# Attention scores as one joint product and two others, sample products over all partitions, and pooling history turned once a tile

## What is computed

```python
xn = rms_norm(h, norm_g)
u, zp, q, k, v, za, ga, gb = split(xn @ w_in)                 # 1024 x 6656
ya = multiscale_pool(concat(pool_prev, u)) * silu(zp)         # windows 2, 4, 8, 16
new_pool = concat(pool_prev, u)[:, -15:]                      # the last 15 rows
q, k = rope(rms_norm(q)), rope(rms_norm(k))                   # 16 query, 4 key heads of 64
o = softmax_with_sink(q @ k.T, window of 128) @ v
m = sigmoid(ga) * (ya @ w_proj_pool) + sigmoid(gb) * ((o * silu(za)) @ w_proj_attn)
h = h + m @ w_out
h = h + sigmoid(h @ w_ple_gate) * (p @ w_ple)
```

## Time and profile before

| | |
|---|---|
| median of 3 runs | 1165.45 us |
| the profiled execution's own time | 1165.09 us |
| its span in the trace | 1163.3 us |
| granted TensorE clock, mean | 0.999 of full |
| busy: PE products | 1156.3 us (99%), 7656 products |
| busy: DVE | 563.9 us (48%) |
| busy: ACT | 395.9 us (34%) |
| busy: POOL | 407.7 us (35%) |

### The profile page before, as it was taken

One profiled execution on the slowest core, in us unless ns is written; L12 is line 12 of the kernel. 1 busy time (PEld: TensorE's weight loads), 2 busy tenths in 40 slices (PEclk: granted clock), 3 DMA queues, 4 the chain that ended last, 5 costly groups with the idle time before them and its releaser, 6 DMA issues.

```text
span 1163.3 us, 20002 instructions
## 1 busy us (share of the span) xinstructions
PE 1156.3 (99%) x7656; PEld 1143.1 (98%) x7656; DVE 563.9 (48%) x1045; ACT 395.9 (34%) x954; POOL 407.7 (35%) x191
## 2 busy tenths in 40 slices
PE   8999999999999999999999999999999999999998
PEld 8999999999999999999999999999999999999998
DVE  5566774112556566564726465832363451163322
ACT  6433334233766767666110010321321030031112
POOL 4433332333212222223333344335432532374310
PEclk9999999999999999999999999999999999999999
DMA  9425466313455555652611111072223232412211
GB/s 303 168 73 149 141 165 181 94 46 87 132 154 158 153 154 134 166 148 74 218 54 51 37 50 36 23 276 76 92 75 124 82 124 77 135 65 64 65 38 56
DMA packets 145791, 130.83 MB, mean 112 GB/s; under 512 B 49039, under 2 KB 134439, under 8 KB 145727
## 3 DMA queue, kind: packets, MB, share of 16 engines
q1 hardware_dynamic: 131063, 106.21, 30.0%
q10 hardware_dynamic: 14664, 23.74, 7.1%
HBM read 94.82 MB, written 37.12 MB: 113 GB/s over the span
## 4 chain that ended last, share of the span: by engine, by line
PE 99%; DMA 1%; SPq 0%; DVE 0%; issue 0%; DVEq 0%
PE ps L684 75%; PE ps L822 11%; PE ps L933 2%; PE ps L708 2%; PE ps L1092 1%; PE ps L964 1%; PE ps L947 1%; PE ps L784 1%; PE ps L698 1%; PE ps L968 1%; PE ps L951 1%; PE ps L1061 1%; DMA xr<-in_x_prompt 1%; PE ps L888 0%; PE ps L868 0%; PE ps L1040 0%
## 5 line engine op out<-in xcount | busy, mean ns | idle before, releaser
L684 PE MATMUL ps<-m_hi,w_hi 128*128 128x352 f32 x1704 | 556.1, 327 | 0.1
L684 PE MATMUL ps<-m_lo,w_hi 128*128 128x352 f32 x1704 | 548.1, 322 | 0.0
L684 PE MATMUL ps<-m_hi,w_lo 128*128 128x352 f32 x1704 | 369.8, 325 | 0.0
L684 PEld LDWEIGHTS ps<-m_hi,w_hi 128*128 128x128 f32 x1704 | 320.9, 188 | 1.3 <-issue 0.5
L684 PEld LDWEIGHTS ps<-m_lo,w_hi 128*128 128x128 f32 x1704 | 320.7, 188 | 0.0
L597 POOL TENSOR_TENSOR w_hi<-raw_a,w_one 128x1024 fp32r<-128x1024 f32 x41 | 78.9, 1923 | 683.4 <-PE ps L684 371.4
L684 PEld LDWEIGHTS ps<-m_hi,w_lo 128*128 128x128 f32 x1704 | 289.8, 188 | 0.0
L599 POOL TENSOR_TENSOR w_lo<-raw_b,w_hi 128x1024 fp32r<-128x1024 f32 x41 | 111.1, 2709 | 3.2
L599 POOL TENSOR_TENSOR w_lo<-raw_a,w_hi 128x1024 fp32r<-128x1024 f32 x41 | 104.1, 2539 | 3.2
L822 PE MATMUL ps<-w_lo,m_hi 128*128 128x256 f32 (+1 forms) x360 | 99.4, 282 | 0.0
L822 PE MATMUL ps<-w_hi,m_hi 128*128 128x256 f32 x320 | 92.3, 288 | 0.0
(11 more groups left out here) (248 smaller groups left out, 1429.9 us busy)
## 6 DMA issues: line engine op xcount, KB each, us to landing
raw_a<-in_w_in SPq DMA_DIRECT2D x25, 512.0 KB, 3.7
raw_b<-in_w_in SPq DMA_DIRECT2D x25, 512.0 KB, 4.6
qk_d<-qkst ACTq DMA_DIRECT2D x20, 512.0 KB, 5.6
gate_d<-gst ACTq DMA_DIRECT2D x16, 528.0 KB, 3.4
gin<-gate_d SPq DMA_DIRECT2D x16, 528.0 KB, 3.6
qt<-qk_d SPq DMA_DIRECT2D x64, 128.0 KB, 3.5
kt<-qk_d SPq DMA_DIRECT2D x96, 64.0 KB, 2.5
vt<-v_d SPq DMA_DIRECT2D x84, 64.0 KB, 2.2
```

Source lines behind the costliest of these rows:

```text
L684: last = nc.tensor.matmul(ps[:, 3 * parity + c, 0:CH], w, x[:, k, CH * c:CH * c + CH], start=(k == 0 and w is wh and x is src_hi), stop=(k ...
```

## The change

Scores: `kt` has two slots by unit parity, each with three planes of 256 tokens: plane 0 holds the high parts of the keys on both halves of the partitions, plane 1 the low parts on the lower half only, plane 2 the low parts on the upper half only; the rest is zero. A new tile `q_high` holds the high parts of q for heads b = 0 on the lower half and b = 1 on the upper half. One product of `q_high` with planes 1 and 2 (2 x 192 columns) replaces the two products with low parts; the two with plane 0 stay. DVE fills `q_high` in a new step `stack_high`, for the next unit, and PE waits for it. DVE's loop over the attention has one pass fewer, which is written out.

Samples: L870 and L885 run over all 128 partitions, with zeros where there was nothing. History: only the 4 new rows of each sample are turned, beside the 15 rows of the prompt, in one transpose; the rows are collected in `kv_flat` and stored at the end by SP; the 11 old rows go from input to output directly. The samples' rows of p are padded to 128 for their transposes.

The diff is cut; the left-out parts are the constants of waits and the matching zero fills on ACT (`v_group`, `spt`, `q_sum`).

```diff
-            kt = sb("kt", [P, NKV, 2, 3, P], F32R, scope=s3)
+            kt = sb("kt", [P, 2, 3, 2 * P], F32R, scope=s3)
+            k_gap = sb("k_gap", [P, 1024], scope=s3)
+            q_high = sb("q_high", [P, 2, 2, 2, HD], F32R, scope=s3)
...
+            sp.dma_start(pool_rows(npool_s)[:, 0:HIST - NT, :], pool_rows(state)[:, NT:HIST, :]).then_inc(out_stored, 16)
...
-                for slot in ((2, 0) if m < 4 else (1,)):
-                    for half in range(2):
-                        sp.dma_start(kt[HD * half:HD * half + HD, kv, :, slot, :].bitcast(F32),
-                                     qk_d[NH + kv, :, tok].rearrange("(s e) n -> e s n", s=2))\
-                            .then_inc(unit_loaded[kv], 16)
+                seen = slice(0, P) if first else bass.ds(t * P - P, 2 * P)
+                for half in range(2):
+                    dst = kt[HD * half:HD * half + HD, m % 2, 0:2 + half:1 + half, P if first else 0:2 * P]
+                    sp.dma_start(dst.bitcast(F32), qk_d[NH + kv, :, seen].rearrange("(s e) n -> e s n", s=2))\
+                        .then_inc(unit_loaded[kv], 16)
...
+            sp.wait_ge(zero_done, 1)
             for m in range(2):
                 load_q_k(m, 0, m)
...
+                sp.wait_ge(pool_copied, KT + 1)
+                sp.dma_start(npool_p, kv_flat[NS:NS + HIST, 0:D]).then_inc(pool_stored, 16)
+                for b in range(NB):
+                    sp.dma_start(pool_rows(npool_s)[b, HIST - NT:HIST, :], kv_flat[NT * b:NT * b + NT, 0:D])\
+                        .then_inc(pool_stored, 16)
...
+                sp.dma_start(yrow[NS:P, PBLK, :], pp[NS:P, :]).then_inc(p_loaded, 16)
...
-                nc.tensor.matmul(ps[:, 7, P:SK], q_sum[0:HD, P * v:P * v + P], k_new[0:HD, NS * v:NS * v + NS],
+                nc.tensor.matmul(ps[:, 7, P:SK], q_sum[:, P * v:P * v + P], k_new[:, NS * v:NS * v + NS],
...
-                nc.tensor.matmul(ps[:, 7, 0:P], v_group[0:NS].rearrange("p s e -> p (s e)"), spt[0:NS, 1, :],
+                nc.tensor.matmul(ps[:, 7, 0:P], v_group[:].rearrange("p s e -> p (s e)"), spt[:, 1, :],
...
+                    pe.wait_ge(q_high_put, u + 1)
                 bank = round_of("S", u, s, m, first)
+                seen = slice(HD * s, HD * s + KW)
+                nc.tensor.matmul(ps[:, bank, :].rearrange("p (b n) -> p b n", b=2)[:, :, 0:KW],
+                                 q_high[:, slot, s, :, :].rearrange("p g n -> p (g n)"), kt[:, slot, 1:3, seen],
+                                 start=True, stop=False)
                 for b in range(2):
-                    for part in range(2):
-                        keys = kt[:, kv, part, :, :].rearrange("p s n -> p (s n)")[:, k0:k0 + KW]
-                        last = nc.tensor.matmul(ps[:, bank, 256 * b:256 * b + KW],
-                                                qt[:, slot, s, 2 * b:2 * b + 2, :].rearrange("p g n -> p (g n)"), keys,
-                                                start=(part == 0), stop=(part == 1))
+                    last = nc.tensor.matmul(ps[:, bank, 256 * b:256 * b + KW],
+                                            qt[:, slot, s, 2 * b:2 * b + 2, :].rearrange("p g n -> p (g n)"),
+                                            kt[:, slot, 0, seen], start=False, stop=(b == 1))
...
-                nc.tensor.transpose(ps[0:nh, 6, 0:P], keep[:, h, :], ident)
-                nc.tensor.transpose(ps[0:HIST, 6, P:2 * P], ub[:, h, SEQ:SEQ + HIST], ident).then_inc(pool_t, 1)
+                nc.tensor.transpose(ps[0:nh, 6, 0:P], keep[:, h, :], ident).then_inc(pool_t, 1)
...
-                    last = nc.tensor.transpose(ps[:, 6 + r % 2, 0:NS], yrow[0:NS, PBLK, P * k:P * k + P],
-                                               ident[0:NS, 0:NS])
+                    last = nc.tensor.transpose(ps[:, 6 + r % 2, 0:P], yrow[:, PBLK, P * k:P * k + P], ident)
...
+            def stack_high(m, t):
+
+                dve.wait_ge(unit_loaded[m % 4], t * 64 + 64)
+                for b in range(2):
+                    last = v.tensor_copy(q_high[HD * b:HD * b + HD, m % 2, :, :, :],
+                                         qt[0:HD, m % 2, :, 2 * b:2 * b + 2, :].bitcast(F32))
+                last.then_inc(q_high_put, 1)
...
-                    v.memset(kt[:, :, :, 1, :].bitcast(F32), 0.0).then_inc(zero_done, 1)
+                    v.memset(kt[:].bitcast(F32), 0.0).then_inc(zero_done, 1)
...
                 step.did(v.memset(sst[:, 0:1], 0.0))
+                if last_group:
+                    stack_high(0, 0)
                 scale_za(kv, 1)
...
                     split_probs(u - 1, (m - 1) % 8)
+                if not (isinstance(i, int) and u == PBLK * NKV - 1):
+                    stack_high((m + 1) % 8, i * 2 + (m + 1) // 4)
                 reciprocals(u, m)
...
-                    ge(dve, pool_t, 2 * g + h - 1)
+                    ge(dve, keep_ready, 2 * g + h - 1)
...
-            dve.wait_ge(pool_stored, 16 * 2 * KT)
...
             scale_gin(0, 5)
+            dve.wait_ge(pool_stored, 16 * (NB + 1))
...
-                ge(act, pool_stored, 32 * (k))
-                a.activation(pst[0:nh, 0, :], ps[0:nh, 6, 0:P], ACT.Copy)
-                a.activation(pst[0:HIST, 1, :], ps[0:HIST, 6, P:2 * P], ACT.Copy).then_inc(pool_copied, 1)
-                act.wait_ge(pool_copied, need + 1)
-                cols = bass.ds(k * P, P)
-                act.dma_start(npool_s[:, cols], pst[0:nh, 0, :]).then_inc(pool_stored, 16)
-                act.dma_start(npool_p[:, cols], pst[0:HIST, 1, :]).then_inc(pool_stored, 16)
+                a.activation(kv_flat[0:NS + HIST, bass.ds(k * P, P)], ps[0:NS + HIST, 6, 0:P], ACT.Copy)\
+                    .then_inc(pool_copied, 1)
```

More of the change, by code:

```diff
@@ L330, in build @@
         att_done, att_read = sem("att_done"), sem("att_read")
-        low_copied, low_added = sem("low_copied"), sem("low_added")
+        low_copied, low_added, q_high_put = sem("low_copied"), sem("low_added"), sem("q_high_put")
         masks_loaded, zero_done = sem("masks_loaded"), sem("zero_done")
@@ L358, in build @@
         v_low, gtmp, sg = kv_out[0:HD, 0, :], kv_flat, rbc
-        pst = kv_out[:, 0, 0:2 * P].rearrange("p (a n) -> p a n", n=P)
         rms_rows = [rows[0:P if t < PBLK else NS, 4, P * t:P * t + P] for t in range(PBLK + 1)]
@@ L382, in _, with pool_rows @@
         def _(sp):
+            def pool_rows(ap):
+                return ap.rearrange("(b h) n -> b h n", h=HIST)
             def load_chunk(n, w, col, extra=None, extra_n=None):
@@ L462, in load_q_k @@
             def load_q_k(u, t, m):
-                tok, kv = bass.ds(t * P, P), m % 4
+                kv = m % 4
                 for a in range(2):
@@ L467, in load_q_k @@
                         .then_inc(unit_loaded[kv], 16)
-                for slot in ((2, 0) if m < 4 else (1,)):
-                    for half in range(2):
-                        sp.dma_start(kt[HD * half:HD * half + HD, kv, :, slot, :].bitcast(F32),
-                                     qk_d[NH + kv, :, tok].rearrange("(s e) n -> e s n", s=2))\
-                            .then_inc(unit_loaded[kv], 16)
+                first = isinstance(t, int) and t == 0
+                seen = slice(0, P) if first else bass.ds(t * P - P, 2 * P)
[3 more added lines that the diff above has]
+                        .then_inc(unit_loaded[kv], 16)
             v_rows = v_d.rearrange("b p v e -> (b p) v e")
@@ L581, in _ @@
             sp.dma_start(y_s[:, 7 * P:8 * P], yrow[0:NS, PBLK, P:2 * P]).then_inc(y_stored[1], 16)
-            sp.wait_ge(out_stored, 16 * (2 * NB + 2 + 2 * NB))
+            sp.wait_ge(out_stored, 16 * (2 * NB + 3 + 2 * NB))
         @block.gpsimd
@@ L919, in round_of, with scores @@
                 return 6 + (att_bank(kind, m, first) + s) % 2
-            def scores(u, m, i, s, first=False):
+            def scores(u, m, t, s, first=False):
                 slot, kv = m % 2, m % 4
@@ L975, in attention_half @@
                 after, between = {k0: [], k0 + 1: [], k0 + 2: [], k0 + 3: []}, {}
-                after[k0].append(lambda: scores(u, m, i, 0, first and m == 0))
-                after[k0 + 1].append(lambda: scores(u, m, i, 1, first and m == 0))
+                after[k0].append(lambda: scores(u, m, t, 0, first and m == 0))
+                after[k0 + 1].append(lambda: scores(u, m, t, 1, first and m == 0))
                 if not first or m >= 1:
@@ L1036, in turn_p @@
                 k, i = divmod(r, 3)
-                pe.wait_ge(p_loaded, 16 * (PBLK + 1))
+                pe.wait_ge(p_loaded, 16 * (PBLK + 2))
                 ge(pe, p_round_free, r - 1)
@@ L1323, in _ @@
             dve.wait_ge(masks_loaded, 16)
-            dve.wait_ge(out_stored, 16 * (2 * NB + 2 + 2 * NB))
+            dve.wait_ge(out_stored, 16 * (2 * NB + 3 + 2 * NB))
             def mask_scores(u, m, start, first):
@@ L1387, in _ @@
                 attention_half(0, m, first=True)
-            with dve.Fori(1, PBLK // 2) as i:
```

(17 more changed lines are left out.)

3 lines of the change are left out of this document (1 added, 2 removed).

## The result

The changed kernel takes 1182.86 us in the median of four executions (1179.02 to 1183.86), the kernel before 1165.12 beside it. The ratio is 1.0145, 95% interval 1.012 to 1.0169: slower by 1.45%, 17.7 us. The profiled execution took 1182.12 us (span 1180.3, granted clock 0.994), 17.0 more than the one of before (1165.09).

A forecast was written before the change was run, and what follows sets the result against it. TensorE, busy 99% of the span, was taken as the bound: 1165.1 - 6.6 gained + 5.0 for held copies + 3.5 for the first pair = 1167.0, plus 0.4 for the median: 1167.5 us, range 1159 to 1182.

The forecast's parts named there:

- double hold: Rival at every fourth unit: POOL wins and queues its next instruction between DVE's two copies; 18.2 us, total 1181.5; chance 0.28.
- the tie: Every fourth unit: POOL's split and DVE's first copy start nearly together, POOL 0.05 ahead; given to neither.
- single hold: Forecast case, every fourth unit: only the second copy waits for POOL; 0.8 each, 0.5 at seams, 5.0 us; 1167.5, chance 0.50.
- the release from DVE's end to PE's start: Delay from the end of DVE's copies to PE's next scores, taken as 0.48 us from L1305 and the scores.
- The first stack_high: First copy pair, after the last sample values, between L1305 and the scores: 0.7 to 4.4 us, taken as 3.5.
- behind L599: Case for the program's first copy pair: it waits for POOL's L599, costing PE 2.7 us.
- The gains: PE time saved: scores 3.1, L870 0.9, L885 1.2, transposes of p 0.5, history 0.9; 6.6 us.
- The round's 0.048: Scores: a round falls from 0.45 to 0.40 us, saving 0.048 in each of 64 rounds, 3.1 us.
- L885's 0.31: Sample product with 32 active rows: full partitions give back 0.31 us, four times, 1.2 us.
- The bare formula: Scores products at columns / 2.4 + 2.5 ns: only 2.5 ns saved each round, 0.16 us in all.
- The parts put at nothing: K loads, state rows, late SP stores, ScalarE's clears, larger kt clear, DVE's store wait: all covered, no cost.
- The signs named: Expected in the profile: 192 scores products, PE waits near 286 and every fourth unit; 3 us waits mean both copies held.

The follow-up runs named there:

- pair_split: Changed kernel, but at every fourth unit the first q_high copy goes between the two parts of the probability split, the second behind it: 1162.77 us, ratio 0.9983.
- act_copies: Changed kernel with q_high copies on ScalarE at each unit's head, first pair on DVE ahead of the last sample product's wait: 1156.58 us, ratio 0.9931.
- four_products: Changed kernel with scores by the four 192-column products of the kernel before, without q_high copies or their wait: 1160.57 us, ratio 0.9964.
- after_again: The changed kernel as it is, measured again beside the kernel before on another chip: 1181.24 us, ratio 1.0147.

## Why the prediction was wrong

It forecast 1167.5 us and a range to 1182; the time was 1182.86, within 1.4 us of the rival of the double hold (1181.5), which had 0.28. The mechanism of that rival is what happened; that its number is so near is partly luck, since it priced the holds at 22.6 us where they cost 18.25, and had no term for the clock, which cost 6.2.

- **The step that failed** is the tie: "that 0.05 ahead is enough no row shows, so I give the tie to neither", and then the chance went nearly two to one to the single hold (0.50 against 0.28), whose 5.0 us stood in the sum. POOL was 0.05 ahead at these places (457.02 against 457.07) and won six of the seven with both of its instructions; the seventh, where DVE was ahead, as the text had it ("0.05 behind once"), was the one single hold. The rows of the tie were right to 0.02 us; the order that they showed should have been followed. Copies asked for 0.03 after the split with POOL 0.02 ahead of the split's end come second, in each of the six.
- **The price of the double hold** was near: 18.2 us for the seven places, 15.95 measured there (2.4 and 2.7 for 2.7 and 3.0). The ends of the copies were right (4.43 after the split for 4.4). Too long was the release from DVE's end to PE's start, 0.48 in the text, which had said that it need not be a pure wait: it took 0.14 (461.47 to 461.61). The whole difference of 0.3 at a place is that. The mechanism, one POOL instruction for each of the two copies, was as described. The Trainium skill (SBUF — State Buffer, Who interferes with whom) has it as an exclusive lock, first come first served; the trace agrees, down to 0.05 us.
- **The price of the single hold** was too high by the same 0.3: 0.8 against 0.47 in the change (2.2 + 0.14 - 1.87), and less in pair_split. Had the tie fallen the other way, the kernel would have been, as an estimate from these sizes, at 1165.1 - 7.7 + 7 x 0.47 + 2.3 = 1163.0 and no slower.
- **The first stack_high** was sized at 3.5 between ends of 0.7 and 4.4; it cost 2.3, the case "behind L599" (2.7) with the same 0.3 off.
- **The gains** were 6.6 by the sum and 7.7 in the trace, 7.9 in act_copies. The round's 0.048 became 0.053. Two errors met there: the new round was put at 0.40 with 0.112 for each small product, where one takes 0.087, and without the 0.02 that the product behind loses as before; with both it is 0.40 again. L885's 0.31 became 0.39: of the sample records on full partitions the 32-column ones take 0.03 from start to start. The bare formula of the Trainium skill (TensorE: Matmul & The Clock Gate, Back-to-back issue gap), by which 0.16 us would have come, is off here by almost 4 us (act_copies against four_products: 4.0); its own warning holds.
- **What was missing altogether** is the clock. The text used 0.999 and never asked what a standstill does to it. It cost 6.2 us in the profiled execution, and put the time past the end of the range: the sum of the double hold with the sizes measured is 1165.1 - 7.7 + 18.25 = 1175.7, and the clock and the 0.1 behind each hold bring it to 1182.
- **The parts put at nothing** (K loads, state copy, late stores, clears) were nothing or nearly so: none has a row among PE's waits, and four_products, which has them all, is faster by 3.9 us, where the starts of its products give 4.3.
- **The signs named** came: waits of 3 us (2.5) at every fourth unit, released by the copy, 192 products on the scores lines, a first wait near 286.

## What to carry to other kernels

A short SBUF copy put on VectorE can cost the GpSimd instruction that runs at that moment, and the next copy the next one: look for the GpSimd instruction that starts within 0.1 us of the new copy's place and take the order of the records at its word. Here both engines hang on PE, and they met in the recorded order at all seven places, with margins of 0.05 and 0.03 us. Before a wait is blamed, see what else stands behind the held instruction on its engine; here most of the loss came back a round later when the wait was gone. Put such a copy on an engine that isn't held (ScalarE, 0.42 us each instead of 2.2), and count standstills of TensorE as long as those here, 2.3 us and more, with a surcharge for the clock. And when a release time is read from the distance of two records, look whether anything was waiting: the 0.48 taken so was 0.14 where PE really waited.

## What the hardware showed that I had not expected

- After a standstill of TensorE of 2.3 to 2.9 us the granted clock sometimes falls to 0.50 for 3.4 us, which costs 1.4 to 1.6 us. Not each does it: the change's profiled execution has seven gaps of that size and four such stretches, and the one of after_again has seven gaps at the same places of the program and one stretch. At 320.1 the clock fell while TensorE still stood, at 286.0 as it came back; at 357.6 it had been at work again for 1.2 us.
- ScalarE's copy of the same 64x256 elements takes 0.40 to 0.42 us with or without GpSimd's split beside it, in all 62 of act_copies.
- Not every SBUF operation of VectorE is held: the reciprocal of four elements at 461.50 runs inside GpSimd's L611 in 0.18 us, its usual time, though it reads and writes SBUF alone.
